# The sliding-window scores of a prompt attention moved ahead of the transposes, in a one-core Trainium2 decoder step

## The reference, cut to what matters

```python
s_c = einsum('bqghd,bngd->bghqn', q, kc) * scale + bias     # compressed keys (63)
p_c = masked_softmax(s_c, cend <= qpos)
s_s = einsum('bqghd,bgqkld->bghqkl', q, k_sel) * scale + bias
p_s = masked_softmax(s_s, tpos <= qp)                       # selected keys
s_w = einsum('bqghd,bkgd->bghqk', q, kw) * scale + bias
p_w = masked_softmax(s_w, (dw >= 0) & (dw <= WINDOW))       # sliding window of 512
o = g[..., 0:1] * (p_c @ vc) + g[..., 1:2] * (p_s @ v_sel) + g[..., 2:3] * (p_w @ vw)
```

## Time and profile before

| what | value |
|---|---|
| three runs | 2184.57, 2187.47, 2188.53 us, median 2187.47 |
| profiled execution | 2183.83 us, its span 2182.1 us |
| PE busy over the span | 93% (matmuls), 13732 of them |
| DVE, ACT, POOL busy | 35%, 23%, 28% |
| granted TensorE clock, mean | 0.961 |
| prompt attention in the span | about 549 to 807 us |

### The profile page before, as it was taken

How to read it: one execution, slowest core, us unless ns; L and a number is a source line. 1 busy time by engine, 2 the same in 40 slices (tenths; PEclk the granted TensorE clock), 3 DMA queues, 4 the chain that set the end, 5 groups by cost and what they waited for, 6 DMA issues and landing times. The chain is left out here.

```text
span 2182.1 us, 33339 instructions
## 1 busy us (share of the span) xinstructions
PE 2039.9 (93%) x13732; PEld 1944.9 (89%) x13732; DVE 754.3 (35%) x1440; ACT 507.6 (23%) x920; POOL 614.6 (28%) x506
## 2 busy tenths in 40 slices
PE   7999999976799989999989899999999999997897
PEld 6999989854688879999989899999999999996886
DVE  4104433233778863122231523012212322334413
ACT  5121011123577771010022311110000000012323
POOL 2323200001445553233332123232233323321110
PEclk9999999977899999999999799999999999998999
DMA  6233354133100011111122311111112112113012
GB/s 236 60 107 106 89 215 155 39 134 158 55 2 2 2 55 44 53 35 53 30 58 105 110 39 43 44 49 48 41 46 58 35 42 58 45 37 125 27 45 81
DMA packets 159027, 150.82 MB, mean 69 GB/s; under 512 B 18712, under 2 KB 151394, under 8 KB 156034
## 3 DMA queue, kind: packets, MB, share of 16 engines
q1 hardware_dynamic: 156082, 111.43, 16.7%
q0 software_dynamic: 2304, 33.56, 3.9%
q10 hardware_dynamic: 528, 4.23, 0.5%
HBM read 132.28 MB, written 21.10 MB: 70 GB/s over the span
## 5 line engine op out<-in xcount | busy, mean ns | idle before, releaser
L573 PE MATMUL ffn_acc<-HH,WS 128*128 128x344 f32 x2112 | 395.8, 322 | 8.4 <-DVE HL L505 7.3
L581 POOL CAST WS<-W 128x1024 fp32r<-128x1024 f32 (+2 forms) x125 | 130.9, 1047 | 901.2 <-PE ffn_acc L573 542.5
L573 PEld LDWEIGHTS ffn_acc<-HH,WS 128*128 128x128 f32 x2112 | 345.0, 189 | 8.8 <-issue 7.3
L583 POOL TENSOR_TENSOR WS<-W,WS 128x1024 fp32r<-128x1024 f32 (+2 forms) x125 | 294.7, 2357 | 10.0
L573 PE MATMUL ffn_acc<-HL,WS 128*128 128x344 f32 x1056 | 225.3, 322 | 0.0
L573 PE MATMUL ffn_acc<-AH,WS 128*128 128x344 f32 x1056 | 195.4, 320 | 0.0
L573 PEld LDWEIGHTS ffn_acc<-HL,WS 128*128 128x128 f32 x1056 | 179.9, 190 | 0.0
L573 PE MATMUL proj_acc<-HH,WS 128*128 128x344 f32 x912 | 174.4, 324 | 5.7 <-DVE HL L505 5.7
L573 PEld LDWEIGHTS ffn_acc<-AH,WS 128*128 128x128 f32 x1056 | 171.7, 188 | 0.0
L573 PEld LDWEIGHTS proj_acc<-HH,WS 128*128 128x128 f32 x912 | 149.0, 189 | 6.6 <-issue 4.1
L573 PE MATMUL merge_acc<-HH,WS 128*128 128x344 f32 x768 | 146.7, 323 | 7.0 <-DVE HL L505 7.0
(11 more groups left out here) (408 smaller groups left out, 3325.5 us busy)
## 6 DMA issues: line engine op xcount, KB each, us to landing
W<-in_w_in SPq DMA_DIRECT2D x30, 512.0 KB, 3.9
W<-in_w_ffn_gate SPq DMA_DIRECT2D x22, 512.0 KB, 3.8
W<-in_w_ffn_up SPq DMA_DIRECT2D x22, 512.0 KB, 3.9
W<-in_w_ffn_down SPq DMA_DIRECT2D x16, 384.0 KB, 3.3
W<-in_w_ffn_down SPq DMA_DIRECT2D x16, 320.0 KB, 3.0
kept_x<-Z SPq DMA_DIRECT2D x1, 4128.0 KB, 13.4
Z<-kept_x SPq DMA_DIRECT2D x1, 4128.0 KB, 14.4
kept_x<-Z ACTq DMA_DIRECT2D x1, 4128.0 KB, 11.6
```

Of the source, the lines that this page charges most:

```text
L573: last = k.nc.tensor.matmul(acc[:, s, n, 0:NW], k.WS[:, ws, part, c, :], src[:, c, n * NW:(n + 1) * NW], start=(c == 0 and part == 0 and s ...
L581: k.nc.gpsimd.tensor_copy(k.WS[:, ws, 0, 0:nk, :], w).then_inc(hi_done, 1)
L583: k.nc.gpsimd.tensor_tensor(k.WS[:, ws, 1, 0:nk, :], w, k.WS[:, ws, 0, 0:nk, :].bitcast(F32), ALU.subtract).then_inc(split_done, 1)
```

## The change

In the loop of PE's program `window_scores(s)` is issued directly behind `selected_scores(s)`, and `turns(s - 2)` stands between it and `products`. Nothing else is touched: the instructions, their waits, the tiles and the programs of the other engines are the same.

```diff
             for s in range(S + 4):
                 if s < S:
                     selected_scores(s)
+                if s < S:
+                    window_scores(s)
                 if 2 <= s < S + 2:
                     turns(s - 2)
-                if s < S:
-                    window_scores(s)
                 if s >= 4:
                     products(s // 2 - 2, s % 2)
```

## The result

The changed kernel takes 2198.39 us (median of 5 runs, 2194.41 to 2204.25) against 2187.47 before: the ratio is 1.0051, 95% interval 1.0032 to 1.0070, or 7 to 15 us slower. Its profiled execution is one of 2198.39 us with a span of 2196.6, 14.6 us more than the profiled one of before. The forecast was 2204.

The account below looks back on a forecast made before the run. PE was taken as the bound in class 3, with some waits in earlier classes. Four quads per class at 0.2, 0.9, 0.3 and 2.7 us gave 16.4 us; on the median 2187.47 that is 2204, range 2190 to 2216.

Parts of the forecast that it names:

- The loop through ACT's queue: Late class 3 steps: W, T, ACT's copies, both exponentials, next W take 4.76 us against 3.92.
- W to T: Term of the class 3 late-step loop: W on PE takes 1.01 us.
- the selected exponentials: Term of the class 3 late-step loop on ACT: 0.80 plus about 0.09 us for the sum's read-out, 0.89.
- E1 and E2 of class 3: E1 takes 4.88 us, by a path over DVE's queries, and E2 4.34; a class 3 quad grows 2.7 us.
- Classes 0 to 2: Quads in these classes lose 0.2, 0.9 and 0.3 us; bounds for each class -0.5 to +1.3 a quad.
- The two late steps: In a quad of classes 1 and 2, loops of 4.49 and 4.38 us make them lose 1.32 and 0.84.
- E2 gives back: Classes 1 and 2: W runs in T's wait for POOL, returning 0.65 us about once a quad.
- What would be late next: DVE's 23.1 us of waiting for W go in part, but ACT's copies are late next; counted as nothing.
- The clock: Rival, chance 0.05: gaps in class 3 lower the clock, up to 2253 us, about 2228 if half shows.
- The sum: Whole stage: 4 x (0.2 + 0.9 + 0.3 + 2.7) = 16.4 us slower.
- no change: Rival, chance 0.09: PE has room, waits fit in; class 3 loses 0.3 us a quad, +1, 2189 us.
- faster: Rival, chance 0.06: W fills T's wait for POOL, 11.7 us less, 2176 us.

Follow-up runs that it names:

- The copies put last in class 3: Changed kernel's order S, W, T, P in class 3 only, ACT's copies there behind both sets of exponentials, old order elsewhere: 2192.01 us, ratio 1.0032.
- the doubled dose: Kernel before with class 3 alone in the order S, W, P, T, so that T stands behind P as well: 2219.83 us, ratio 1.0153.
- late copies: Kernel before, old PE order; in class 3 ACT waits for the end of the same step's W before its copies: 2197.18 us, ratio 1.0046.
- the queries split: Changed kernel with DVE's queries in two halves, at the ends of E1 and L1: 2210.98 us, ratio 1.0110.
- the complement: Kernel before with W ahead of T in the first 48 steps, old order in class 3: 2190.03 us, ratio 1.0019.
- class 3 alone: Kernel before with W ahead of T in the last 16 steps only (class 3): 2197.58 us, ratio 1.0048.
- W in E2: Kernel before with W ahead of T only in step E2 of classes 0 to 2: 2183.87 us, ratio 0.9995.
- copies last in the old order: Kernel before, old PE order everywhere, in class 3 ACT's copies behind both sets of exponentials: 2206.20 us, ratio 1.0097.

## Why the prediction held, and where it was off

- **The loop through ACT's queue.** Right. The changed kernel's rows show it term by term: late steps of class 3 take 4.61 us (772.50 to 777.11) where 4.76 was forecast. Two terms were too large: W to T is 0.94, not 1.01, and the selected exponentials 0.77, not 0.89, since half a read-out was added that overlaps. The copies put last in class 3, and the doubled dose in its steps at the upper clock, show that the copies' place and T's lateness set the loop; the late copies in the old order cost as much, over another loop.
- **E1 and E2 of class 3.** E1 4.98 us (777.11 to 782.09) for 4.88, E2 4.17 for 4.34. The path of E1 is the forecast one: DVE's queries stand between L2's selected exponentials and E1's minima, and with the queries split E1 fell to 4.18. The quad is 2.2 us longer, for 2.7.
- **Classes 0 to 2.** 0.3, 0.5 and 0.05 us a quad for 0.2, 0.9 and 0.3. For classes 1 and 2 the sums were too large, and their parts were off both ways. This is a quad of class 1, by the starts of S in E1, E2, L1, L2 and the next E1, first before the change, then after:

```profile
640.37 0.38 PE L1710 MATMUL att_slc<-KH,QT 128*128 128x256 f32 x1
...
643.62 0.39 PE L1710 MATMUL att_slc<-KH,QT 128*128 128x256 f32 x1
...
647.61 0.50 PE L1710 MATMUL att_slc<-KH,QT 128*128 128x512 f32 x1
...
651.47 0.51 PE L1710 MATMUL att_slc<-KH,QT 128*128 128x512 f32 x1
...
655.55 0.39 PE L1710 MATMUL att_slc<-KH,QT 128*128 128x256 f32 x1
```

```profile
644.18 0.36 PE L1710 MATMUL att_slc<-KH,QT 128*128 128x256 f32 x1
...
647.91 0.39 PE L1710 MATMUL att_slc<-KH,QT 128*128 128x256 f32 x1
...
651.40 0.50 PE L1710 MATMUL att_slc<-KH,QT 128*128 128x512 f32 x1 [0.23 <-ACT Hr L1788]
...
655.48 0.50 PE L1710 MATMUL att_slc<-KH,QT 128*128 128x512 f32 x1
...
659.92 0.36 PE L1710 MATMUL att_slc<-KH,QT 128*128 128x256 f32 x1
```

E1 grows by 0.48 us and E2 shrinks by 0.50, L1 grows by 0.22 and L2 by 0.36. The two late steps lose 0.6 where 1.32 was forecast: their loop was put at 4.49 us and takes 4.2 to 4.4, and it was compared with a mean step of 3.83, though a late step took 3.9 to 4.1 before. E1's loss was put at 0.2. In class 2 the late steps lose 0.5 for 0.84, E1 loses 0.5, and E2 gives back 0.9, more than the 0.65 that was taken: with the waits for the other tile, which were not read, T waits 4.7 us for POOL in these four quads, 1.2 in each.

- **What would be late next.** Of DVE's 23.1 us of waiting for W all but 1.7 went, and it bought nothing, as said: in step 55 DVE's minima are ready before ACT comes to them.
- **The clock.** Its rival was placed in class 3, where nothing of it shows in the changed kernel. The clock acted in the first two quads, which the prediction left out: 2.4 us in the profiles, of which about 1.5 are the change's (last section). The stretches that the prediction reads for it hold transposes among matmuls; no run here has a long stretch of transposes alone.
- **The sum.** 16.4 was forecast; the profiled executions differ by 14.6, the medians by 10.9, and the interval reaches to 15: the sum was somewhat too large. Classes 1 to 3 were put at 15.6 us and take 10.6; that the profiles come as near as 14.6 is in part luck, since the 2.4 us at the start belong to no term of the sum. The rivals "no change" and "faster" fell with the waits that W and ACT now show: PE does have room in class 3 (18.2 of 20 us busy), and it helps nothing. The price of "faster" was read too low as well, 11.7 us where T's whole wait for POOL was 16.8.

## What to carry to other kernels

When work is moved within one engine's program, ask first who waits for what is now issued later: here waits of W on PE, of 0.2 to 1.2 us, came with 2.2 us more in a quad, because another engine's in-order queue had the delayed result at its head and the release of that wait at its tail. Add up that loop from the durations of the trace, release to release, and compare it with the bound engine's own work per step; what is longer sets the pace. Before a cure by reordering the second engine, look for every buffer that its work frees.

## What was not expected of the hardware

The granted clock at the start of the stage. Two-us rows of the changed kernel:

```profile
560.00:562.00 2.00, 2.00 (x8) 1.61 (x6) 1.24 (x2) 0.07 (x1) 0.17 (x1) 0.50 0.00 0
...
564.00:566.00 2.00, 1.00 (x10) 0.88 (x9) 1.94 (x4) 1.07 (x4) 1.17 (x1) 1.00 0.00 0
566.00:568.00 2.00, 2.00 (x13) 1.98 (x11) 1.85 (x11) 1.20 (x3) 0.21 (x1) 0.53 0.03 8
```

In this profile it rose to the upper of its two levels, 2.4 GHz, at about 562.5 us, some 4 us later than in the profile before the change (558 to 560 us had 0.98 there), fell to 1.2 GHz again at 566 us after two waits of PE, 0.82 us before the S of 563.71 and 1.00 before the W of 565.12, and rose anew. From the first S to the ninth step it took 31.5 us here and in the complement, 29.0 to 30.2 in six profiles that keep the old order in these steps or nearly (the kernel before, class 3 alone, W in E2, late copies, and the two with copies last in class 3).

The late rise isn't the change's. In three of these six (class 3 alone, late copies, and copies last in the old order) the clock rises about 13 us after the first S, as in the changed kernel, and in the other three 8 to 9 us after it. Class 3 alone, whose first S starts at 551.12:

```profile
562.00:564.00 2.00, 2.00 (x9) 1.76 (x8) 1.53 (x4) 0.26 (x3) 0.33 (x2) 0.50 0.00 0
564.00:566.00 2.00, 1.14 (x10) 1.06 (x10) 1.50 (x10) 1.20 (x3) 1.22 (x2) 0.93 0.00 0
```

The first quad takes 14.15 or 14.16 us in those three and in the changed kernel, 13.27 to 13.29 in the others, so 0.9 of the 2.4 us comes and goes with the same program. The second fall shows in no profile with the old order in these steps; in the changed kernel and the complement the second quad takes 17.34 and 17.39 us, against 15.75 to 15.99 in the six. These 1.5 us go with the change, in two profiles.

With the selected exponentials first on ACT the clock fell repeatedly through class 0 (0.51 in 570 to 580 us), and quads took up to 20.9 us. In class 3 of the changed kernel waits of PE of up to 1.6 us did not bring it down; in the doubled dose, with waits of up to 1.6 us and more of them, it fell there three times. That the fall follows the gaps is read from these rows; no run held the gaps and varied the rest.
